# RWKV block inverse: the level product of a step and the updates of the step behind it form one piece of the matmul engine's order

## The reference

```python
def step(S, inp):
    w_t, k_t, v_t, a_t, b_t = inp[:5]
    sa = jnp.einsum('dbhij,dbhj->dbhi', S, a_t)
    S = S * w_t[..., None, :] + sa[..., :, None] * b_t[..., None, :] + v_t[..., :, None] * k_t[..., None, :]
    return S, (jnp.einsum('dbhij,dbhj->dbhi', S, inp[5]) if with_out else None)
```

## Time and profile before

| | |
|---|---|
| median of 3 runs | 2883.95 us (2872.29 to 2889.89) |
| profiled execution | 2875.47 us, its span 2873.7 us |
| busy share of the span | PE 89%, weight loads 72%, VectorE 38%, ScalarE 33%, GpSimd 20% |
| chain that ended last | PE 81%, VectorE 9%, issue 5%, ScalarE 4%, DMA 1% |

### The profile page before, as it was taken

The page is one execution under the profiler, slowest core; times in us unless marked ns, Lnnn a source line. Parts: engine busy times, 40 slices in busy tenths (PEclk is TensorE's granted clock), DMA queues, the critical chain, the costliest instruction groups (busy, mean ns, idle before and its releaser), DMA issues.

```text
span 2873.7 us, 68057 instructions
## 1 busy us (share of the span) xinstructions
PE 2545.0 (89%) x28963; PEld 2078.8 (72%) x28963; DVE 1092.0 (38%) x2296; ACT 952.6 (33%) x1600; POOL 573.7 (20%) x361
## 2 busy tenths in 40 slices
PE   4975999989999999599858999999999986899998
PEld 2852777768888888488636877777777774688886
DVE  3015555423121112342453655655655553212211
ACT  3146555423131212322333333333343332323323
POOL 0311000113222322012401111111111111244441
PEclk8986999999999999899978998989889895999999
DMA  5310444311211211023300000000000001132321
GB/s 195 81 44 31 161 162 150 87 43 59 73 58 58 73 58 58 30 77 103 106 27 20 11 13 20 11 13 20 11 13 11 12 3 47 60 114 88 101 88 59
DMA packets 172286, 176.05 MB, mean 61 GB/s; under 512 B 26240, under 2 KB 159760, under 8 KB 172048
## 3 DMA queue, kind: packets, MB, share of 16 engines
q1 hardware_dynamic: 172048, 172.49, 19.0%
HBM read 160.93 MB, written 11.53 MB: 60 GB/s over the span
## 4 chain that ended last, share of the span: by engine, by line
PE 81%; DVE 9%; issue 5%; ACT 4%; DMA 1%; SPq 0%; POOL 0%; DVEq 0%; ACTq 0%
PE PS L376 45%; PE PS L1086 5%; PE PS L549 2%; PE PS L1071 2%; PE PS L900 2%; PE PS L409 2%; PE PS L576 2%; PE PS L843 2%; PE PS L850 2%; PE PS L1066 1%; PE PS L1190 1%; PE PS L1166 1%; PE PS L1178 1%; PE PS L530 1%; PE PS L836 1%
## 5 line engine op out<-in xcount | busy, mean ns | idle before, releaser
L356 POOL TENSOR_TENSOR WL<-RAW,WH 128x1024 fp32r<-128x1024 f32 x184 | 440.4, 2416 | 1381.2 <-ACT WH L350 1381.2
L376 PE MATMUL PS<-AH,WH 128*128 128x256 f32 (+1 forms) x1512 | 540.8, 358 | 105.8 <-POOL WL L356 52.3
L376 PE MATMUL PS<-AH,WL 128*128 128x256 f32 (+1 forms) x1512 | 539.3, 357 | 0.0
L376 PE MATMUL PS<-AL,WH 128*128 128x256 f32 (+1 forms) x1512 | 534.7, 354 | 0.0
L376 PEld LDWEIGHTS PS<-AH,WH 128*128 128x128 f32 x1512 | 290.6, 192 | 157.2 <-issue 74.5
L376 PEld LDWEIGHTS PS<-AL,WH 128*128 128x128 f32 x1512 | 289.2, 191 | 41.4
L376 PEld LDWEIGHTS PS<-AH,WL 128*128 128x128 f32 x1512 | 290.3, 192 | 37.4
L350 ACT ACTIVATE WH<-RAW 128x1024 fp32r<-128x1024 f32 x184 | 183.9, 1048 | 394.0 <-PE PS L376 392.5
L376 PE MATMUL PS<-BH,WL 128*128 128x512 f32 (+1 forms) x768 | 273.7, 356 | 0.0
L376 PE MATMUL PS<-BH,WH 128*128 128x512 f32 (+1 forms) x768 | 272.9, 355 | 0.0
L376 PE MATMUL PS<-BL,WH 128*128 128x512 f32 (+1 forms) x768 | 271.8, 354 | 0.0
(11 more groups left out here) (221 smaller groups left out, 4221.5 us busy)
## 6 DMA issues: line engine op xcount, KB each, us to landing
ADW<-l_ada_w SPq DMA_DIRECT2D x40, 1024.0 KB, 5.1
RAW<-l_mlp_up SPq DMA_DIRECT2D x64, 512.0 KB, 4.3
RAW<-l_mlp_down SPq DMA_DIRECT2D x64, 512.0 KB, 4.0
RAW<-l_w_rkv SPq DMA_DIRECT2D x24, 512.0 KB, 4.6
rwkv_scratch<-STG SPq DMA_DIRECT2D x24, 384.0 KB, 2.7
ADA<-l_ada_w SPq DMA_DIRECT2D x4, 2048.0 KB, 19.1
RAW<-l_w_in SPq DMA_DIRECT2D x16, 256.0 KB, 4.4
RAW<-l_w_out SPq DMA_DIRECT2D x16, 256.0 KB, 5.0
```

The costliest lines, as they stand in the source:

```text
L356: e.tensor_tensor(WL[:, s, rows], RAW[:, s, rows], WH[:, s, rows], ALU.subtract).then_inc(w_split[h], 1)
L376: mm = e.matmul(dst, w[:, s, k, n * P:(n + 1) * P], r[:, k, lo:hi], start=(k == 0 and i == 0), stop=(k == KT - 1 and i == 2), skip_group_c ...
```

## The change

The `yield` between level product and updates is taken away, and a second one is put at the end of a step. The 8 matmuls of P and the 16 of U become one piece, and the next i of the string finds an empty piece. Only the generator of the matmul engine is changed; VectorE, ScalarE, GpSimd and the DMA queues keep their order. No instruction and no wait is added or removed.

```diff
                     mm.then_inc(u_done, 1)
-                yield
                 if n >= 4:
                     v = n - 1
...
                     mm.then_inc(inv_done, 1)
+                yield
                 yield
```

## The result

The changed kernel takes 2912.64 us in the median (four runs, 2903.01 to 2914.45) against 2882.59 us before: ratio 1.010, with an interval of 1.0061 to 1.0139. Timed a second time beside other kernels (experiment 1) it came to 1.0115 (1.0093 to 1.0136). So it is slower by 30 to 33 us. The forecast was 2903 us, in a range from 2877 to 2935; the measured median lies in the range, 9.6 us above the forecast. The profiled execution took 2903.01 us, 27.5 us more than that of before.

A forecast was written before the change was run, and what follows sets the result against it. PE's order was taken to bound the kernel, each chain gap costing the larger of work and VectorE round trip. Terms 75 - 40 - 10 gave +25 us: 2900 on the profiled execution, 2909 on the median; forecast 2903 us, range 2877 to 2935.

The forecast's parts named there:

- The rule: Between two chain pieces on PE, a gap costs the larger of its work and the chain's round trip over VectorE.
- C1 to C2: Gap between these chain pieces on PE: 8 us more where U enters, 12 us less where U leaves.
- U enters: PE gaps between chain pieces that U newly joins cost more, 75 us in sum; 0.48 us each in a full gap.
- U leaves: PE gaps between chain pieces that lose U give back 40 us in sum, partly because VectorE's mask then runs under U.
- C3 to C1: Gap between these chain pieces on PE: 25 us more where U enters, 6 us less where U leaves.
- with preparation: Chain gaps also holding preparation work: full, so U costs 24 us where it enters and gives back 20 us where it leaves.
- "Issue": PE's waits for nothing the profile shows, 20.6 us at U: they stay, but half, 10 us, falls into idle gaps.
- ScalarE's copies: U waits for the copies of the U before; costed at 0, at most 4 us, in even slots U10 to U11.
- Faster: Rival: VectorE gains more than gaps lose, at gaps U leaves; -6 us, 2878 on the median; chance 0.08.
- No difference: Rival: round trips are hidden anyway or savings equal costs; 0 to 8 us, 2884 to 2892; chance 0.24.
- Prices without hiding: Rival: the gap prices hold, but none of the "issue" waits is covered; +35 us, 2919; chance 0.18.
- The clock: Rival: bare chain pieces bring more stretches at the lower clock, 8 to 30 us on top, up to 2935; chance 0.12.

The follow-up runs named there:

- experiment 1: The same change timed once more against the kernel before: 2913.24 us against 2880.24, ratio 1.0115.
- Experiment 2: Only half of U (8 of 16 matmuls) joins P, the other half stays in U's old place, against the kernel before: 2895.80 us, ratio 1.0064.
- experiment 7: Kernel before, with VectorE doing P's mask after RH or the new state where C1 or C3 stands right behind P: 2878.66 us, ratio 1.0002.
- experiment 3: One joined piece as in the change, but U first and P behind it, against the kernel before: 2974.54 us, ratio 1.0339.
- 9 and 10: The change with ScalarE's copies of updates moved up one piece, in the second all but the last step's: 2921.04 us (1.0142) and 2917.99 us (1.0134).
- experiment 6: The change with all chain pieces behind the others at each slot's end: 3355.92 us, ratio 1.1663 to the kernel before; same order without the change 3322.82 us.
- 9 to 12: 9 and 10, then two against the kernel before: even slots' string changed, P and U apart, ratio 1.0016; P and U joined only at picked steps, 1.0037.
- experiment 9: The change with ScalarE's copies of updates moved up one piece, against the kernel before: 2921.04 us, ratio 1.0142.

## Why the prediction came out right, step by step

**The rule holds for most gaps.** Waits for RH, SA and SS together should grow from 19.7 to over 50 us: they are 66.1, by the same rows. Slots 2 to 15 should take near 802 us: they took 798.0, and 811.5 in experiment 1. The clock over them stays within 0.02. Bare C2 to C3 should take 1.00: in the same slot C2.4 starts at 1742.03 and C3.4 at 1743.02, 0.99 us. Two signs were met in part. Bare C1 to C2 should take 0.80 us and RH should leave the mask: it is 0.79 in most gaps, but 1.31 to 1.39 in 14 of 54, where VectorE had the preparation's work ahead of both. The prediction took the round trip for a constant; it contains what stands in VectorE's queue. And P with U between C2 and C3 should take 1.48 us: the 8 gaps that had both before still take 1.48, the 24 in which U is new take 1.22 in the median.

The terms, as forecast and as the sums over the gaps:

| gaps | U enters, forecast | measured | U leaves, forecast | measured |
|---|---|---|---|---|
| C1 to C2 | 8 | 20.0 | 12 | 9.3 |
| C2 to C3 | 18 | 11.4 | 2 | 4.3 |
| C3 to C1 | 25 | 24.6 | 6 | 8.8 |
| with preparation | 24 | 30.0 | 20 | 23.8 |
| sum | 75 | 86 | 40 | 46 |

**U enters.** U in a full gap was taken at 0.48 us; C3 to C1 gives 0.47 in the medians (0.47 to 0.94). C1 to C2 is too small by 12 us, but not for its price of 0.21 us a gap: 9.9 us lie in the 8 gaps from C1.6 to C2.6 of the even slots (0.70 to 1.98 us), where U8 waits for ScalarE (below), and the other 23 gaps of the later chunks took 0.26 each. C2 to C3 was taken too high: 0.45 a gap, against 0.26 in 24 gaps and 0.34 in the 15 of the first chunks. The gaps with preparation took more: C2 to C3 with mat and P +11.4 in 21 gaps, 0.54 each.

**U leaves.** The mask's price was right in kind. 0.18 us a gap stood in the sum for C1 to C2, the middle between 0 and 0.36, because two cases were thought to alternate. The medians fell by 0.26, and by 0.24 in C3 to C1, but the mean over the 69 gaps is 0.13, since in 14 of them the mask stays ahead and in others there was nothing to win. Experiment 2 shows that the gain is the mask's, and experiment 7 that taking it by deferring the mask costs as much elsewhere.

**"Issue": 10 forecast.** The term spoke of the two rows of U, 20.6 us. They are 13.5 + 1.1 = 14.6 us after, 6.0 less. Over all lines of the RWKV stage it is 39.6 us in 59 times before and 19.8 in 26 after, with the same instructions, and 24.9 in experiment 1 with the same kernel. So these waits don't come with the number of instructions alone, as the prediction had it, and half of them are left, not none. Experiments with more idle time of PE have fewer: 17.0 us in experiment 3, 13.3 and 14 in 9 and 10. These rows are in the gap means above and can't be added to them; how much of them was hidden and how much never arose isn't known.

**ScalarE's copies: 0 forecast, at most 4, and 5 us of waits measured,** and the place was wrong. I had named U10 to U11; it is U8, in each even slot from 2 to 14. The timeline of the kernel after:
```profile
2036.62 0.87 PE L867 MATMUL PS<-CK,VG 128*128 128x128 f32 x6
...
2037.53 0.81 ACT L950 ACTIVATE VT<-PS 128x768 f32<-128x768 f32 x1 [2.77 <-PE PS L867]
...
2038.24 0.38 ACT L1116 ACTIVATE XI<-PS 128x256 f32<-128x256 f32 x1
...
2038.50 0.39 ACT L1118 ACTIVATE XIT<-PS 128x256 f32<-128x256 f32 x1
...
2038.99 0.24 PE L1066 MATMUL PS<-UM,XIT 64*64 64x64 f32 x1 [0.77 <-ACT XIT L1118]
```
U7 used to stand behind vt and now stands ahead of it. But ScalarE's own order still has the copy of vt, 0.81 us, ahead of the copies of U7, and that copy waits for the matmuls of vt. Between vt and U8 stood U7, C1, P9 and C2, and now only C1 and P9. P9 to P10 took 3.36 us instead of 2.06 in the median of the seven even slots, of which 5.0 / 7 = 0.7 stand in this wait. With the 0.22 us that the busy time hides of each, it is 5.0 + 7 x 0.22 = 6.5 us by estimate, the largest part of what the 86 us are over 75. That is the term that the prediction had wrong: it looked at what lies on PE between two U, and not at what stands ahead of their copies in ScalarE's queue.

**The sum** was 75 - 40 - 10 = +25 us. Measured over the gaps, in which "issue" and ScalarE are contained, it is 86 - 46 - 6 = +34, of which the shorter chain pieces take 7.7; the chain's stretch grew by 27.1, the execution by 27.5, the medians by 30 to 33. Two terms that were too small on opposite sides, and two small ones that weren't in the sum (the other gaps, the chain pieces), nearly cancel: the sign and the order of size were worked out, that +25 came within a few us of 27.5 is luck. The forecast itself was set at 2903 us, 6 below the 2909 that the sum gives on the median; the measured median, 2912.64, is nearer to 2909 than to 2903, and its step of 30 us stands at the upper edge of the +9 to +30 of the forecast.

**The rivals.** *Faster* had its condition nearly met, the mask right ahead of RH in 68 of the 90 gaps from C1 to C2, and fell by its price: all 121 gaps gave back 28 us, with what U itself cost beside the preparation, and not 44. *No difference* fell with ratio 1.010: 8 us were its most, and the interval begins at 17.6. *Prices without hiding*, +35 or 2919 us, came nearer to the timed median (6 us off) than the forecast did (10 off). Its reason, that no "issue" is covered, isn't what the rows show: they lost 15 to 20 us over all lines. *The clock* is not the cause here: slots 1 to 16 have 0.89 in both kernels. It moved between slots, though: slot 16 fell from 0.92 to 0.77 and is the one that is 5.1 us longer, while slots 2 to 15 rose. Experiment 3 shows the rival as real: there the clock over slots 1 to 16 fell to 0.83, worth up to 66 of the 73 us that they grew over the change.

**What stays open.** How the waits for "issue" arise. The splits of experiment 3 between mask and clock, and of experiment 6 between round trips and clock, are bounds. That the term of the copies can be mended was not shown: both attempts lost more elsewhere.

## What to carry to other kernels

Where a chain on one engine makes round trips over another, a gap costs the larger of the work in it and the round trip, and the round trip contains what stands ahead in the other engine's queue; here one piece in each of two gaps was cheaper than two pieces in one and none in the other, though no instruction was added. Price single gaps to judge the sign of a regrouping, but don't expect the price of one to survive when it is moved alone: with several in-order queues the waits come back in other places (experiments 7, 9 to 12). When a piece moves on one engine, read the order of each engine that serves it, for what stands ahead of its copy there.

## What the runs showed of the hardware that was not expected

The waits for "issue" depend on the order of the instructions, not on their number only: 39.6 us in 59 times in the RWKV stage before, 19.8 in 26 after (24.9 in 35 in experiment 1), 13.3 in experiment 9.

A wait of 1.24 us in a stretch in which PE was busy for 1.45 of 2.90 us was followed by 10.6 us at a granted clock of 0.52 (experiment 3). At the same step of the changed kernel (here in slot 10), with a wait of 0.77 us, PE was busy for 2.38 of 3.50 us, and nothing of the kind followed; its windows, around 2038.99 and then the next 10 us:
```profile
2037.50:2041.00 3.50, 2.38 (x81) 2.16 (x83) 2.45 (x7) 2.02 (x5) 0.00 (x0) 1.00 0.03 7
2041.00:2051.00 10.00, 8.28 (x267) 7.38 (x261) 7.99 (x19) 4.67 (x11) 0.00 (x0) 1.00 0.02 3
```
So half a microsecond of idle time more can stand ahead of a stretch at half the clock that costs several microseconds; that it alone brings the fall isn't shown, since in three of the seven even slots of experiment 3 the clock fell ahead of this wait. In the listing of a sum of gaps such a stretch looks like a gap that became twice as long for no reason of its own; the granted clock beside it tells.
